# One sum per token for the expert outputs, filled by two 64-row accumulating scatters per block, one after the other

## The reference, cut to what matters

```python
h = jax.nn.silu(jnp.einsum('td,edf->tef', xt, wg)) * jnp.einsum('td,edf->tef', xt, wu)
routed = jnp.einsum('tef,efd->td', h * gates[..., None].astype(h.dtype), wd)   # 64 experts, 8 gates per token are not 0
...
xc = xc + g2 * moe(...)          # routed + shared
y_prompt = rms_norm(xc, final_norm_g)
```

## Time and profile before

| | |
|---|---|
| median of 3 runs | 1784.59 us (1780.01 to 1786.79) |
| the profiled execution | 1785.4 us, its span 1783.6 us |
| mean granted TensorE clock | 0.916 of full speed |
| TensorE busy over the span | 1547.1 us (87%) |
| VectorE, ScalarE, GpSimd busy | 776.8, 503.0, 588.7 us |
| DMA moved | 289.50 MB, mean 162 GB/s |
| `experts` | about 1058 to 1705 us of the span |
| `combine` | 1710.8 to 1783.6 us of the span |

### The profile page before, as it was taken

How to read it: one execution, slowest core, us unless ns; L and a number is a source line. 1 busy time by engine, 2 the same in 40 slices (tenths; PEclk the granted TensorE clock), 3 DMA queues, 4 the chain that set the end, 5 groups by cost and what they waited for, 6 DMA issues and landing times. The chain is left out here.

```text
span 1783.6 us, 28574 instructions
## 1 busy us (share of the span) xinstructions
PE 1547.1 (87%) x9111; PEld 918.0 (51%) x9112; DVE 776.8 (44%) x1497; ACT 503.0 (28%) x1141; POOL 588.7 (33%) x612
## 2 busy tenths in 40 slices
PE   5999999656663899999989869999989999999745
PEld 2654445445452687845555535555545555555411
DVE  2300000266746555528877324444434444444329
ACT  2300000143324455211110003433333343333312
POOL 0000000176650521011112643555545555555422
PEclk8999999856576899999999989999999999999968
DMA  8220000000002981410200029999999999996467
GB/s 318 77 94 0 24 0 3 14 1 7 1 1 67 414 348 47 167 68 30 100 25 1 0 96 300 333 339 330 341 341 342 332 330 296 277 263 138 74 247 307
DMA packets 93495, 289.50 MB, mean 162 GB/s; under 512 B 12190, under 2 KB 15602, under 8 KB 93170
## 3 DMA queue, kind: packets, MB, share of 16 engines
q1 hardware_dynamic: 66210, 199.96, 29.2%
q0 software_dynamic: 25920, 83.91, 19.6%
q10 hardware_dynamic: 1296, 4.72, 0.7%
HBM read 222.09 MB, written 76.94 MB: 168 GB/s over the span
## 5 line engine op out<-in xcount | busy, mean ns | idle before, releaser
L1914 PE MATMUL ps_g<-w_exp,mix 128*64 x1408 | 326.3, 385 | 5.6 <-DVE own_gu L2009 2.8
L1917 PE MATMUL ps_g<-own_gu,mix 128*64 128x256 f32 x1408 | 326.4, 385 | 0.0
L1914 PEld LDWEIGHTS ps_g<-w_exp,mix 128*64 128x64 f32 x1408 | 187.2, 138 | 107.6 <-issue 10.8
L230 PE MATMUL psP<-wring,hT 128*128 128x512 f32 (+1 forms) x576 | 216.7, 539 | 0.0
L1863 POOL DMA_INDIRECT sum_rows<-mix,scatter_row x66 | 144.1, 2184 | 172.1 <-DVE mix L1952 146.2
L1917 PEld LDWEIGHTS ps_g<-own_gu,mix 128*64 128x64 f32 x1408 | 187.2, 138 | 0.0
L1886 PE MATMUL ps_y<-w_exp,hidT 128*64 x352 | 171.6, 610 | 6.2 <-ACT own_d L1965 6.2
L1887 PE MATMUL ps_y<-own_d,hidT 128*64 128x512 f32 x352 | 171.6, 610 | 0.0
L230 PEld LDWEIGHTS psP<-wring,hT 128*128 128x128 f32 x576 | 109.4, 190 | 107.6 <-issue 103.9
L2009 DVE COPY own_gu<-w_exp 128x2048 f32 x89 | 109.3, 1228 | 57.1 <-issue 42.2
L1288 PE MATMUL ps_o<-wo,mixT 128*128 128x512 f32 x288 | 125.2, 592 | 0.5 <-DVE h L1541 0.5
(11 more groups left out here) (313 smaller groups left out, 2564.3 us busy)
## 6 DMA issues: line engine op xcount, KB each, us to landing
w_exp<-in_exp_w_gate SPq DMA_DIRECT2D x64, 512.0 KB
w_exp<-in_exp_w_up SPq DMA_DIRECT2D x64, 512.0 KB
w_exp<-in_exp_w_down SPq DMA_DIRECT2D x64, 512.0 KB
sum_rows<-zero_row SPq DMA_DIRECT2D x10, 2048.0 KB
sums<-sum_rows SPq DMA_DIRECT2D x36, 512.0 KB
ada_ring<-in_w_ada SPq DMA_DIRECT2D x8, 2048.0 KB
wring<-in_w_ada SPq DMA_DIRECT2D x4, 2048.0 KB
wring<-in_w_in SPq DMA_DIRECT2D x4, 2048.0 KB
```

The lines of the kernel that those rows point to most:

```text
L230: last = pe.matmul(bank, hT[:, j, t * P:(t + 1) * P], w[:, j, 0:what[1]], start=(j == 0), stop=(j == KD - 1))
L1914: pe.matmul(ps_g[par][0:HALF, 0:2 * FF].rearrange("p (k f) -> p k f", k=2), xT[par][:, j * P:j * P + HALF], w[:, bass.ds(slot * 3, 2), ff] ...
L1917: last = pe.matmul(ps_g[par][HALF:P, 0:2 * FF].rearrange("p (k f) -> p k f", k=2), xT[par][:, j * P + HALF:(j + 1) * P], own_gu[par][:, :, ...
```

## The change: what it does

`sum_rows` becomes one tensor of 1280 rows: one sum per token. A block leaves in two scatters of 64 rows, the low half and then the high half. Each is issued only when the former one has landed: GpSimd waits for the high half of the block before (`y_out`), issues the low half, gathers for the block four ahead, waits for the low half (`y_low`), and issues the high half. `write_table` copies the row numbers of the high half to partitions 0 to 63 (column 3), so that both scatters read their indices there. The gather of a block, first in the loop before, now stands between the two scatters. The zeroing shrinks from ten DMAs of 2 MB to two of 2.5 MB. `combine` loads one row of sums per tile (9 DMAs, all tiles resident), and neither TensorE nor GpSimd works there any more.

```diff
@@ window_attention, SP
-                for k in range(*((2 * i, 2 * i + 2) if i < 2 else (i + 2, i + 3))):
-                    rows = dram["y"][k % 2].rearrange("(p t) n -> p t n", p=P)[:, 4 * (k // 2):4 * (k // 2) + 4, :]
-                    sp.dma_start(rows, zero[:].unsqueeze(1).to_broadcast([P, 4, D])).then_inc(sums_zero, 16)
-            sp.wait_ge(sums_zero, 160)
+                if 5 * i < SUM_ROWS // P:
+                    rows = dram["y"].rearrange("(p t) n -> p t n", p=P)[:, 5 * i:5 * i + 5, :]
+                    sp.dma_start(rows, zero[:].unsqueeze(1).to_broadcast([P, 5, D])).then_inc(sums_zero, 16)
+            sp.wait_ge(sums_zero, 32)
@@ write_table
+                dve.tensor_copy(tab[0:HALF, :, 3], tab[HALF:P, :, 1])
@@ experts, GpSimd
-        si = [sb(f"scatter_row{i}", [P, 1], I32) for i in range(4)]
+        si = [sb(f"scatter_row{i}", [HALF, 2], I32) for i in range(4)]
+            def scatter(k, half, landed):
+                pool.indirect_dma_start(out=dram["y"], out_offset=bass.IndirectOffsetOnAxis(ap=si[k][:, half:half + 1], axis=0),
+                                        in_=y[k][half * HALF:(half + 1) * HALF, :], in_offset=None,
+                                        bounds_check=SUM_ROWS - 1, compute_op=ALU.add).then_inc(landed, 16)
...
-                    pool.wait_ge(xT_done, b + 1)
-                    pool.sem_inc(passed, 1)
-                    gather(k, b + 4)
-                    if not first(i):
-
-                        pool.wait_ge(y_out[k], i * 16)
-                        pool.sem_inc(passed, 1)
-                    if not (first(i) and k < 2):
-
-                        pool.wait_ge(y_out[(k + 2) % 4], (i + k // 2) * 16)
-                        pool.sem_inc(passed, 1)
-                    pool.tensor_copy(si[k][:], keep["tab"][:, b, 1:2]).then_inc(si_done, 1)
+                    if not (first(i) and k == 0):
+
+                        pool.wait_ge(y_out[(k + 3) % 4], (i + (k > 0)) * 16)
+                        pool.sem_inc(passed, 1)
+                    pool.tensor_copy(si[k][:], keep["tab"][0:HALF, b, 1:4:2]).then_inc(si_done, 1)
                     pool.wait_ge(si_done, b + 1)
                     pool.wait_ge(y_act, b + 1)
                     pool.wait_ge(y_dve, b + 1)
                     pool.sem_inc(passed, 1)
-                    pool.indirect_dma_start(out=dram["y"][k % 2], out_offset=bass.IndirectOffsetOnAxis(ap=si[k][:], axis=0),
-                                            in_=y[k], in_offset=None,
-                                            bounds_check=2 * SUM_ROWS - 1, compute_op=ALU.add).then_inc(y_out[k], 16)
+                    scatter(k, 0, y_low[k])
+
+                    pool.wait_ge(xT_done, b + 1)
+                    pool.sem_inc(passed, 1)
+                    gather(k, b + 4)
+
+                    pool.wait_ge(y_low[k], (i + 1) * 16)
+                    pool.sem_inc(passed, 1)
+                    scatter(k, 1, y_out[k])
@@ combine: SP; the blocks of TensorE and GpSimd are gone
-                for i in range(NS):
-                    at = SUM_ROWS * (i // 2) + t * P
-                    sp.dma_start(sums[:, t % NB, i, :], dram["y"][i % 2][at:at + P, :]).then_inc(sum_in[t % NB], 16)
+                sp.dma_start(sums[:, t, :], dram["y"][t * P:(t + 1) * P, :]).then_inc(sum_in[t], 16)
@@ combine, VectorE, total(t)
-                dve.tensor_tensor(r[t % 2][:, H:D], s[:, 0, :], s[:, 1, :], ALU.add).then_inc(g_done, 1)
-                dve.wait_ge(low_done, t + 1)
-                dve.tensor_tensor(r[t % 2][:, 0:H], ps_r[t % 2][:], g2[:, 0:H], ALU.mult)
-                dve.wait_ge(g_done, 2 * t + 1)
-                dve.tensor_tensor(r[t % 2][:, H:D], r[t % 2][:, H:D], g2[:, H:D], ALU.mult).then_inc(g_done, 1)
-                dve.wait_ge(g_done, 2 * t + 2)
+                dve.wait_ge(sum_in[t], 16)
+                dve.tensor_tensor(r[t % 2][:], sums[:, t, :], keep["g2"][:, cond_of(t), :], ALU.mult).then_inc(g_done, 1)
+                dve.wait_ge(g_done, t + 1)
                 dve.tensor_tensor(keep["x1"][:, t, :], keep["x1"][:, t, :], r[t % 2][:], ALU.add).then_inc(x_done, 1)
```

More of the change, by code:

```diff
@@ L1754, in experts @@
         x_in = [sem(f"x5_in{i}") for i in range(4)]
+        y_low = [sem(f"y_low{i}") for i in range(4)]
         y_out = [sem(f"y_out{i}") for i in range(4)]
@@ L2038, in sem @@
             return nc.alloc_semaphore(name)
[L2040 to L2043, removed]
+        sums = sb("sums7", [P, NT, D])
         r = [sb(f"r7_{i}", [P, D]) for i in range(2)]
@@ L2050, in combine @@
         rstd = sb("rstd7", [P, NT])
[L2051 to L2055, removed]
+        sum_in, fg_in = [sem(f"sum_in{t}") for t in range(NT)], sem("fg_in")
+        g_done, x_done, ssq_done, std_done, rstd_done, out_done = (
+            sem("g7_done"), sem("x7_done"), sem("ssq7_done"), sem("std7_done"), sem("rstd7_done"), sem("out7_done"))
         stored = [sem(f"stored{i}") for i in range(2)]
@@ L2061, in _ @@
             for t in range(NT):
-                if t >= NB:
-                    sp.wait_ge(low_done, t - NB + 1)
-                    sp.wait_ge(g_done, 2 * (t - NB + 1))
-                for i in range(NS):
-                    at = SUM_ROWS * (i // 2) + t * P
-                    sp.dma_start(sums[:, t % NB, i, :], dram["y"][i % 2][at:at + P, :]).then_inc(sum_in[t % NB], 16)
+                sp.dma_start(sums[:, t, :], dram["y"][t * P:(t + 1) * P, :]).then_inc(sum_in[t], 16)
                 if t == 1:
                     sp.dma_start(fg[:], dram["final_g"].to_broadcast([P, D])).then_inc(fg_in, 16)
[L2071 to L2086, removed]
         @block.vector
@@ L2090, in total @@
             def total(t):
-                s = sums[:, t % NB, :, H:D]
-                g2 = keep["g2"][:, cond_of(t), :]
-                dve.wait_ge(high_done, t + 1)
-                dve.tensor_tensor(r[t % 2][:, H:D], s[:, 0, :], s[:, 1, :], ALU.add).then_inc(g_done, 1)
-                dve.wait_ge(low_done, t + 1)
-                dve.tensor_tensor(r[t % 2][:, 0:H], ps_r[t % 2][:], g2[:, 0:H], ALU.mult)
-                dve.wait_ge(g_done, 2 * t + 1)
-                dve.tensor_tensor(r[t % 2][:, H:D], r[t % 2][:, H:D], g2[:, H:D], ALU.mult).then_inc(g_done, 1)
-                dve.wait_ge(g_done, 2 * t + 2)
+                dve.wait_ge(sum_in[t], 16)
+                dve.tensor_tensor(r[t % 2][:], sums[:, t, :], keep["g2"][:, cond_of(t), :], ALU.mult).then_inc(g_done, 1)
+                dve.wait_ge(g_done, t + 1)
                 dve.tensor_tensor(keep["x1"][:, t, :], keep["x1"][:, t, :], r[t % 2][:], ALU.add).then_inc(x_done, 1)
@@ L2151, in program @@
         dram["h2"] = nc.dram_tensor("h2_rows", (T, D), F32, kind="Internal").ap()
-        dram["y"] = [nc.dram_tensor(f"sum_rows{i}", (2 * SUM_ROWS, D), F32, kind="Internal").ap() for i in range(2)]
+        dram["y"] = nc.dram_tensor("sum_rows", (SUM_ROWS, D), F32, kind="Internal").ap()
         def stage(build):
@@ L2214, in route_columns @@
     cols = [t * P + slot + 1 for t in range(NT)]
-    cols += [T + slot % HALF + 1, SUM_ROWS * (slot // HALF) - 1, 2 * slot, 2 * slot + 1]
+    cols += [T + slot % HALF + 1, slot * 0 - 1, 2 * slot, 2 * slot + 1]
     return np.stack(cols, 1).astype(np.float32)
```

## The result

The changed kernel takes 2292.7 us (2286.5 to 2298.1, 4 runs) against 1785.4 (4 runs of before), a ratio of 1.285 with a 95% interval of 1.282 to 1.287. That lies in the predicted range (2040 to 2360) and in the predicted direction; the point forecast of 2150 is 143 us too low. The profiled execution took 2295.9 us, its span is 2294.1.

What follows compares the result with a forecast made beforehand. It took TensorE to bound the experts' stage before and the chain of scatter landings after: 1785.4 + 395.0 (experts) − 28.3 (combine) − 1 (zeroing) = 2151.1, predicted as 2150 us, range 2040 to 2360.

Steps and rivals of the forecast that it cites:

- What bounds the stage, and what would bound it after: Experts' stage: TensorE bounds it before at 6.82 us a block; after, GpSimd's chain of landings at 11.5 us, +395.0 us.
- The way: Experts' stage: from a landing to the next scatter's start, 1.15 us before low and 0.95 before high, 2.1 a block.
- Where TensorE would stand waiting: Experts' stage: TensorE's down product waits for output buffers to be moved, idle for 4.7 us of each 11.5.
- The lone landing: Experts' stage: a 64-row scatter without other traffic lands after 3.5 to 4.8 us, taken as 4.2.
- The 5.95 us for a lone whole: Time in flight of the earlier kernel's last 128-row scatter, alone, from its start at 1698.65 to 1704.6.
- The writing: GpSimd's descriptor writing for a 64-row scatter: between 0.8 and 2.1 us; low descriptors taken as out 1.2 us in.
- Crowding: Experts' stage: other DMA load adds 0.5 us to each half's landing, making it 4.7 us.
- Combine: End of the kernel: VectorE sets the pace, 4.1 us a tile in place of 6.30; 44.5 us against 72.8, −28.3 us.
- Zeroing: Before the experts: 15 MB less written while TensorE is busy; −1 us, between 0 and −3.
- TensorE's clock: Rival, 12%, experts' stage: idle TensorE's clock falls; only half speed throughout binds, 13.64 us a block, time 2340.
- Halves that cost as much as wholes: Rival, 15%, experts' stage: each half lands in 5.95 us, 14.0 us a block, 2370 us; at 6.5 us each 2467.
- Quick landings: Rival, 4%, experts' stage: a half lands in 2.6 us, 7.3 us a block, time 1782, no change.

Runs made afterwards that it cites:

- e3: The changed kernel, but from the fifth block on a gather brings 16 rows and not 128: 2295.3 us.
- e11: The changed kernel with weights after the eighth expert at 128 columns, later gathers at 16 rows, VectorE's copy of the high half's weights at 256 columns: 2155.2 us.
- e2: The changed kernel, but after the first eight experts each weight load brings 128 of 1024 columns: 2169.3 us.
- e1: The changed kernel with the gather issued again at the head of a block, before the low scatter: 2286.2 us.
- e7: The kernel before with the changed kernel's combine, reading only one of the four sums: 1755.2 us.
- e9: The kernel before, but in combine TensorE adds the four sums for 768 columns, VectorE for the other 256, GpSimd does nothing: 1785.0 us.
- e5: The kernel before with each whole 128-row scatter issued only when that of the block before has landed: 1935.2 us.
- e10: The changed kernel with weights after the eighth expert at an eighth of the columns and gathers from the fifth block on at 16 rows: 2203.3 us.
- e8: The kernel before, but in combine TensorE adds the four sums of all 1024 columns and GpSimd does nothing: 1795.3 us.

## Why the prediction was right in kind and 143 us short

- **What bounds the stage, and what would bound it after: right.** 88 blocks of two landings and 2.1 us on the way. The way measured: over all blocks the scatters start 6.71 us (low to high) and 6.46 us (high to low) apart, of which 0.83 and 1.30 us lie behind the landing, 2.14 in all before rounding. Where TensorE would stand waiting was wrong: not at the output buffers but at the gathers, which come at the same pace (e3).
- **The lone landing: the term that was too small.** I took 4.2 us, the rows say 4.7 (e11), 0.5 us twice in each of 88 blocks: 88 us of the 143. What failed are the two ends. I had put 0.15 us between the writing and the first data, and nothing behind the last. In the last scatter of the changed kernel 0.57 us pass before the first data, and 0.35 us between the last data (2245.83) and the landing (2246.18). The cause is a misread view: the earlier trace rows counts a packet where it starts, so that its first packets, of the stretch 1700.40 to 1702.00, seemed to follow the writing at once. A finer stretch shows none before 1700.80:

```profile
1700.40:1700.80 0.40, 0.00 (x0) 0.00 (x0) 0.00 (x0) 0.00 (x0) 0.00 (x0) 1.00 0.00 0
1700.80:1701.00 0.20, 0.00 (x0) 0.00 (x0) 0.00 (x0) 0.00 (x0) 0.00 (x0) 0.78 5.36 328
```

  The 5.95 us for a lone whole is short for the same reason: by the trace's semaphore records it landed at 1705.05, after 6.4 us. Two smaller errors went the other way, so that the sum was off by 0.5 us a landing where its missing ends are 0.8; that was luck. The transfer was 2.4 us and not 2.5. The writing was 1.41, where 4.2 − 2.5 − 0.15 leaves 1.55 for it; the prediction's 1.2, used for the gather, does not fit its own sum.
- **Crowding: right in kind, too small.** 0.5 us per landing was taken, (13.17 − 11.56) / 2 = 0.8 us measured, 53 us over the stage. Nearly all goes with the weights (e2, 0.7 us), and most of the rest with VectorE's copy on descriptor writing. It falls mostly on one half: in the changed kernel a low half lands after 5.9 us in the mean and a high one after 5.2 (the distances 6.71 and 6.46, less the way). In e1, with the gather ahead of the low scatter, it is 5.0 and 5.8. That the gather would be out of the way was right (e1).
- **Combine: −28.3 predicted, −30.2 in the trace, −29.6 alone (e7).** A tile takes 3.8 and not 4.1 us. But that VectorE alone set the pace before was half the story: e9 takes GpSimd's part off it and gains nothing, for the 18.9 MB of loads end at 1768.5 and TensorE's 5.4 us come behind them. The change gains since it takes away both.
- **Zeroing: −1 predicted, 0.** The first scatter starts at 1088.70 in both.
- **The rivals.** TensorE's clock did fall, to 0.79 in the stretch shown, and did not bind: a block needs about 6.82 / 0.79 = 8.6 us and has 13.17. Halves that cost as much as wholes: no, 4.5 against 5.9 us at the minimum, though much nearer to a whole than to half of one. Nor do 64 rows leave engines idle: the lone half has a DMA share of 0.92 from 2244 to 2245. Quick landings: none came under 4.3 us in any run. By the Trainium skill's fit ("DMA: Bandwidth & Descriptors", "Anatomy of one DMA — SWDGE (gpsimd) path") a half would have landed in 2.6 us; for an accumulating scatter the trace does not agree.

Open: why weights crowd the landings by 1.4 us a block on average. Their loads are released by TensorE, which is released by the gather, and the traces show that they fall at a phase of the block: the middle half of them is issued 0.9 to 3.7 us after the low scatter's start in the changed kernel, where low halves land late. In e1 it is 5.2 to 7.5 us, where the high scatter starts at 5.9 and high halves land late. Whether another order on SP would let them miss the scatters wasn't tried.

## What to carry to other kernels

As long as transfers overlap and nothing waits for them, their latency costs nothing, as in the kernel before. Before ordering them one behind another, put a price on a landing from issue to semaphore (here 4.5 us for 262 KB and 5.9 for 524 KB, so two halves cost far more than a whole) and multiply it by how often the chain turns. A new wait shows up in the profile wherever the slowed pace reaches the busiest engine first, here at a gather that was innocent: make that transfer small and see if the time falls. Fewer bytes and fewer instructions pay only where they are on the path; the 30 us in `combine` were real, and about an eighteenth of what the experts' stage lost.

## What the runs showed of the hardware that was not expected

- Writing the descriptors of an accumulating indirect DMA takes GpSimd 1.41 us for 64 rows (changed kernel, e11) and 1.61 us for 128 (e5): most of it does not depend on the rows.
- The same writing takes 0.56 us longer in the mean, up to 1.0, when VectorE's 128x2048 SBUF copy lies on it (e10). In the kernel before, 81 of 88 scatters overlap the copy and take 2.21 us in the mean, the other seven 1.61; that is the median of 2.1 in the earlier trace rows. A change of phase between two instructions that share no data went with 34 us more (e10 against e2), and cutting the copy took 48 us off (e11 against e10).
- A lone half of 64 rows (262 KB) spends 1.4 us on descriptor writing, 0.57 until the first data, 2.3 to 2.4 on the transfer and 0.35 until the semaphore (the changed kernel's last scatter, and in e11 the medians of the 68 high halves whose packets can be told apart). About half of it is not transfer.
- An identity matmul of 512 columns in float32 costs TensorE 0.89 us in the mean (two instructions of 0.44 in the profile), so adding four sums of 1024 columns takes 7.1 us a tile, more than VectorE's work on a tile before, 6.3 us (e8).
